# Expert weights of a decoder layer read with matrix row k*128+p in partition p instead of row p*16+k

## The reference, cut to what matters

```python
a = jnp.einsum('td,edf->tef', t, w_gate)      # t: (256, 2048), w_gate: (32, 2048, 512)
u = jnp.einsum('td,edf->tef', t, w_up)        # w_up: (32, 2048, 512)
act = jax.nn.silu(a) * u * combine[:, :, None]
y = jnp.einsum('tef,efd->td', act, w_down)    # w_down: (32, 512, 2048)
```

## Time and profile before

| | us |
|---|---|
| median of 3 runs | 1414.9 |
| lowest and highest run | 1414.54 and 1415.96 |
| the profiled execution, its own time | 1417.27 |
| its span in the trace | 1415.4 |
| TensorE busy | 1070.2 (76%) |
| VectorE busy | 535.7 (38%) |
| ScalarE busy | 335.8 (24%) |
| HBM read | 479.04 MB |

### The profile page before, as it was taken

One profiled execution on the slowest core, in us unless ns is written; L12 is line 12 of the kernel. 1 busy time (PEld: TensorE's weight loads), 2 busy tenths in 40 slices (PEclk: granted clock), 3 DMA queues, 4 the chain that ended last, 5 costly groups with the idle time before them and its releaser, 6 DMA issues.

```text
span 1415.4 us, 21595 instructions
## 1 busy us (share of the span) xinstructions
PE 1070.2 (76%) x8742; PEld 641.4 (45%) x8742; DVE 535.7 (38%) x1111; ACT 335.8 (24%) x605; POOL 33.2 (2%) x95
## 2 busy tenths in 40 slices
PE   7999999999999978656576565765667656676655
PEld 6888887878887733222232222322223222232221
DVE  5455576566665523222222222222222222222222
ACT  5554456665455300000000000000000000000002
POOL 1000000110001000000000000000000000000001
PEclk9999999999999999987889878898788887888888
DMA  7776663325556999999999999999999999999996
GB/s 228 248 210 182 179 171 108 95 84 187 185 179 210 427 421 422 428 426 427 424 426 427 428 424 425 426 429 426 427 425 426 428 426 427 424 425 427 427 425 272
DMA packets 87779, 481.69 MB, mean 340 GB/s; under 512 B 11382, under 2 KB 21756, under 8 KB 54588
## 3 DMA queue, kind: packets, MB, share of 16 engines
q1 hardware_dynamic: 87244, 478.75, 84.6%
q10 hardware_dynamic: 304, 2.11, 0.4%
q0 software_dynamic: 192, 0.31, 0.2%
HBM read 479.04 MB, written 2.10 MB: 340 GB/s over the span
## 4 chain that ended last, share of the span: by engine, by line
DMA 43%; PE 37%; SPq 6%; ACT 5%; DVE 3%; issue 2%; POOL 0%; ACTq 0%; POOLq 0%; DVEq 0%
DMA gu<-in_w_up 42%; PE ps L504 6%; PE ps L506 6%; PE ps L505 6%; PE ps L878 5%; SPq L388 5%; PE ps L936 4%; PE ps L859 2%; DMA down<-in_w_down 2%; DVE w_lo L1365 1%; SPq L398 1%; PE ps L867 1%; ACT x_slots L1291 1%; ACT w_hi L1009 1%; PE ps L471 1%
## 5 line engine op out<-in xcount | busy, mean ns | idle before, releaser
L878 PE MATMUL ps<-gu,xe 128*32 128x256 f32 x4096 | 316.8, 478 | 240.5 <-DMA gu<-in_w_up 239.9
L878 PEld LDWEIGHTS ps<-gu,xe 128*32 128x32 f32 x4096 | 154.3, 136 | 423.8 <-DMA gu<-in_w_up 287.1
L1817 DVE TENSOR_TENSOR x_res<-ps,x_res 128x512 f32<-128x512 f32 x248 | 154.0, 684 | 412.5 <-PE ps L890 412.5
L1365 DVE TENSOR_TENSOR w_lo<-w_raw,w_hi 128x1024 fp32r<-128x1024 f32 (+1 forms) x138 | 164.2, 1200 | 133.2 <-ACT w_hi L1009 130.1
L504 PE MATMUL ps<-w_hi,a_hi 128*128 128x512 f32 (+1 forms) x480 | 189.9, 396 | 3.8 <-DVE w_lo L1365 3.8
L505 PE MATMUL ps<-w_lo,a_hi 128*128 128x512 f32 (+1 forms) x480 | 185.9, 387 | 0.0
L506 PE MATMUL ps<-w_hi,a_lo 128*128 128x512 f32 (+1 forms) x464 | 179.1, 386 | 0.0
L1009 ACT ACTIVATE w_hi<-w_raw 128x1024 fp32r<-128x1024 f32 (+1 forms) x138 | 141.8, 1039 | 132.1 <-PE ps L506 114.0
L1298 ACT ACTIVATE sg<-ps 128x128 f32<-128x128 f32 x31 | 8.6, 278 | 608.1 <-PE ps L878 608.1
L936 PE MATMUL ps<-down,turned 128*32 128x512 f32 x1024 | 120.0, 606 | 29.7 <-ACT turned L1304 23.6
L504 PEld LDWEIGHTS ps<-w_hi,a_hi 128*128 128x128 f32 x480 | 91.1, 190 | 23.6 <-issue 5.5
(11 more groups left out here) (296 smaller groups left out, 831.0 us busy)
## 6 DMA issues: line engine op xcount, KB each, us to landing
down<-in_w_down SPq DMA_DIRECT2D x128, 1024.0 KB, 23.6
gu<-in_w_gate SPq DMA_DIRECT2D x63, 2048.0 KB, 31.6
gu<-in_w_up SPq DMA_DIRECT2D x63, 2048.0 KB, 36.0
w_raw<-in_w_in SPq DMA_DIRECT2D x56, 512.0 KB, 4.4
w_raw<-in_w_out SPq DMA_DIRECT2D x32, 512.0 KB, 4.0
w_raw<-in_w_mem_kv SPq DMA_DIRECT2D x16, 512.0 KB, 4.1
w_raw<-in_w_mem_q SPq DMA_DIRECT2D x8, 512.0 KB, 3.5
w_raw<-in_w_mem_o SPq DMA_DIRECT2D x8, 512.0 KB, 3.6
```

Of the source, the lines that this page charges most:

```text
L878: mm = pe.matmul(ps[5][j * SLOTS:(j + 1) * SLOTS, 0:2 * P].rearrange("s (m f) -> s m f", m=2), xe[:, k, :], gu[side][:, b, :, kk, j * P:(j ...
L1365: ve.tensor_tensor(w_lo[:, u % RING, :, 0:n], w_raw[:, u % RING, :, 0:n], w_hi[:, u % RING, :, 0:n], ALU.subtract).then_inc(S("w_split"), 1)
L1817: ins = ve.tensor_tensor(xs, ps[g][:, :], xs, ALU.add)
```

## The change

The gate and up weights are loaded with matrix row k*128+p as the k-th of partition p. The amount of data and the place of a half in `gu` stay; in HBM a half is now eight runs of 2 KB, 256 KB apart, and neighbouring partitions read neighbouring runs. The gather of the first expert reads 512 consecutive elements of `x_res`, `h_nat` is made without a step, and the gain comes from `g_t`, so `g_ffn`, its load and VectorE's wait for it are gone. The order of all other instructions on every engine is as before.

```diff
-        g_ffn = place("g_ffn", [P, KD])
...
-                sp.dma_start(g_ffn[:, :], norm_ffn[0].rearrange("(p k) -> p k", k=KD)).then_inc(
-                    S("ffn_gain_loaded"), 16)
...
-                wg = w_gate[0, e].rearrange("(p k) f -> p (k f)", k=KD)
-                wu = w_up[0, e].rearrange("(p k) f -> p (k f)", k=KD)
-                half = KD // 2 * FE
+                wg = w_gate[0, e].rearrange("(k p) f -> p k f", p=P)
+                wu = w_up[0, e].rearrange("(k p) f -> p k f", p=P)
+                half = KD // 2
...
-                        sp.dma_start(gu[side][:, b, m].rearrange("p k f -> p (k f)"),
-                                     w[:, b * half:(b + 1) * half]).then_inc(
+                        sp.dma_start(gu[side][:, b, m], w[:, b * half:(b + 1) * half, :]).then_inc(
...
-                    sp.dma_start(gu[0][:, 0, m, k0:k1, :].rearrange("p k f -> p (k f)"),
-                                 w[0, 2].rearrange("(p k) f -> p (k f)", k=KD)[:, k0 * FE:k1 * FE]
-                                 ).then_inc(S("gu_loaded00"), 16)
+                    sp.dma_start(gu[0][:, 0, m, k0:k1, :],
+                                 w[0, 2].rearrange("(k p) f -> p k f", p=P)[:, k0:k1, :]).then_inc(S("gu_loaded00"), 16)
...
-                            h, rows = hot_0[:, t, :], x_res[:, t, :].rearrange(
-                                "q (p k) -> q k p", k=KD)[:, 4 * g:4 * g + 4, :]
+                            h, rows = hot_0[:, t, :], x_res[:, t, g * UN:(g + 1) * UN]
...
-                sc.activation(h_nat[:, t], x_res[:, t, :].rearrange("q (p k) -> q k p", k=KD), ACT.Copy,
+                sc.activation(h_nat[:, t], x_res[:, t, :].rearrange("q (k p) -> q k p", k=KD), ACT.Copy,
...
-                    gb = g_ffn[:, 4 * g:4 * g + 4].rearrange("p (k a) -> p k a", a=1)
+                    gb = g_t[:, 70 + 4 * g:74 + 4 * g].rearrange("p (k a) -> p k a", a=1)
...
-            ve.wait_ge(S("ffn_gain_loaded"), 16)
```

## The result

The changed kernel takes 1460.25 us (median of 4 runs, 1459.54 to 1461.03), the kernel before 1415.43 us on the same chip. The ratio is 1.0314, with an interval of 1.0299 to 1.0328: it is 44 us slower. The predicted time was 1453.3 us, in a range of 1438 to 1480. The span of the profiled execution is 1458.2 us, 42.8 us longer than before.

The account below looks back on a forecast made before the run. Full DMA engines moving the expert weights were taken as the bound. Run length +38.7 and g_ffn -0.3 us gave 1455.7 from the profiled 1417.27, or 1414.9 + 38.4 = 1453.3 us for the median; range 1438 to 1480.

Parts of the forecast that it names:

- The bound: Experts, from 446.5 us: they last as long as their bytes take on 16 full DMA engines, 29.5 us each.
- The run length: Gate and up loads: 268.4 MB in 2 KB runs at 404 GB/s instead of 429, 38.7 us more.
- the edge of the range: Gate and up loads: a milder slowdown to 390 GB/s, +62.6 us, was put as the slow limit.
- the pattern in HBM: Gate and up loads: 2 KB pieces side by side for neighbouring partitions, the k-th 256 KB on, were given no price.
- g_ffn: SP's queue at the start: without this load's issue the ring's fifth unit goes earlier, -0.3 us.
- The first gather and h_nat: First expert's gather 1.7 us shorter and ScalarE's copies perhaps half, but the gain is covered by the queue: 0.
- SP and the queue: SP's issue of 2 MB loads with 1024 runs: generating runs keeps ahead six times over, cost 0.
- B: Gate and up between 448 and 1387 us: 2 KB runs keep full rate, 429 GB/s, 1414.6 us; chance 0.06.
- estimate of 26 us: Gate and up packets: 3 cycles of overhead each, 67 cycles for 2 KB and 515 for 16 KB; about 26 us more.
- rival C: Gate and up: long packets like those between 5 and 9 us return, 330 to 398 GB/s, +49 to +188 us; chance 0.16.
- A: Gate and up: short runs' overhead partly hidden in a full queue, 410 to 424 GB/s, +7 to +29 us; chance 0.12.
- D: First gather or start of transfers shortens the path and run length costs nothing: 1413 us or less; chance 0.02.

Follow-up runs that it names:

- the one with the old loads: The changed kernel with gate and up loaded as before (row p*16+k in partition p, 16 KB runs), new gather kept, no g_ffn: 1409.77 us, ratio 0.9949.

## Why the prediction was right, and where it was not

**The bound.** Right. From 446.5 to 1440 us the share is 1.04 at 407 GB/s, and the kernel's end follows the rate. The first gate load is issued at 446.16 us, at 446.47 before.

**The run length, +38.7 us.** Right in mechanism, too small. Between the changed kernel and the one with the old loads, at the changed kernel's addresses, it is (1.0314 - 0.9949) x 1415 = 52 us. The term that was mis-sized is this one, by the choice of its row: 404 GB/s, from four microseconds at the start, was taken for the rate of 2 KB runs, and the rate depends on the destination's address, which that step did not weigh. In the changed kernel one side of `gu` runs at 409 GB/s and the other at 387. With all addresses good the cost is 34.5 us, between the bounds of 408 and 404; at the addresses of the kernel before it is 1483.4 - 1415.5 = 68 us, beyond the edge of the range. That the pattern in HBM has no price was right (1483.43 against 1483.34 us).

**g_ffn, -0.3 us.** Wrong, by a cause that the step did not contain: 6 to 8 us with the old loads (0.9949 against 1.0004 with the 64 bytes back), 23 us with the new. Its load, its wait and its place in SP's queue are worth nothing, as said; its 64 bytes are. The two errors have opposite signs, +13 and -7 us against the forecast of 38.4, and leave 44. With the 64 bytes kept, the change of the runs alone would have taken 1483.4 us, outside the range. So the mechanism was right, but that the time fell inside the range was in part luck: it rests on an effect that the prediction did not contain.

**The first gather and h_nat, 0.** Right. The gather takes 1.92 us instead of 3.62, the two copies 3.90 instead of 7.46 us, the first piece for expert 2 is issued at 489.86 instead of 493.02 us, and the kernel with these and the old addresses stands at 1.0004.

**SP and the queue, 0.** Right. SP stands up to 12.7 us in one issue, and with loads cut in two the time is the same. The share of 1.04 shows no gap.

**The rivals.** B, that 2 KB cost nothing, is refuted, and with it, for this kernel, the Trainium skill's 512 bytes as the least transfer for line rate ("DMA: Bandwidth & Descriptors", "Specifications"): over whole experts, 2 KB at good addresses reach 415 GB/s where 16 KB reach 430. The prediction's estimate of 26 us from the 3 cycles of the Trainium skill ("DMA: Bandwidth & Descriptors", "Why small descriptors are slow (HBM only)") comes to 25 when it is worked out again, as 435 x 512 / 515 is 432.5 and not 432.7; the 34.5 us measured at good addresses are more. The long packets of the first microseconds (rival C, 310 GB/s) did not come back: the lowest full slice of the experts is 398. A has nothing for it, as gate and up weights alone run at 409 GB/s at best, and D has nothing either.

**What stays open.** The second side of `gu` at 128 bytes behind a multiple of 256 is slow, and moving it cures it. But the ring's loads and x, whose destinations are also 128 behind a multiple, run at 404 GB/s between 9 and 13 us in the changed kernel and at 406 with everything at multiples of 256:

```profile
9.00:13.00 4.00, 3.55 (x8) 2.81 (x9) 2.32 (x4) 1.06 (x1) 0.00 (x0) 1.00 1.05 406
```

That is hardly slower, and I don't know why it isn't. It is also the reason why the row that I had taken looked better than gate and up weights could be at the old addresses. Whether a conflict with what the engines read and write at the same time plays a part was not tried.

## What to carry to other kernels

Where the 16 DMA engines are full, count packets: a layout that splits each run of 16 KB into eight of 2 KB cost 4.8 ns for each further packet of an engine, 34.5 us here with destinations at multiples of 256 bytes, and nothing that the compute engines gained could pay for it. A removed tile is also a moved tile: before a difference of half a per cent is put down to an instruction, look at which large tiles' addresses changed, and put the bytes back as a control. Large load destinations at multiples of 256 bytes gave 7 us here with no edit but the addresses.

## What the runs showed of the hardware that was not expected

- A shift of 64 or of 128 bytes of the expert weights' destination away from a multiple of 256 lowered the rate of full DMA engines: from 415 to 398 GB/s with 2 KB packets for gate and up (409 to 387 for these alone), from 430 to 426 GB/s with 16 and 8 KB packets. The ring's loads did not show it (404 against 406).
- A load whose rows follow one another in HBM was cut into packets by the destination too: 2 KB pieces interleaved on the memory side of the core gave as many packets as 2 KB runs in HBM, and the same 398 GB/s at the same addresses.
- With shorter runs SP stands in the issue while fewer bytes are under way: with eight times the runs the time from issue to landing of the up weights fell from 36 to 19.9 us, and the median issue of a 2 MB load took SP 5309 ns instead of 1201, at no cost that the share of 1.04 would show. What limits the queue was not isolated. A rough estimate fits neither a fixed number of bytes nor one of runs: 36 us at 426 GB/s are 15 MB or some 900 runs of 16 KB, 19.9 us at 408 GB/s are 8 MB or some 4000 runs of 2 KB.
- A step of two float32 in the moving operand cost TensorE little: the shortest instruction of `gate_up` took 385 instead of 376 ns. (The medians, 393 and 379 ns, tell less, since the changed kernel has 397 without a step.) A step of 16 cost much: 3.62 us for 16 instructions, 1.92 without it.
